# Two-layer transformer kernel: the delta rule's sums over the head dimension as two fp32r products each, and the first block's calls in a new order

## What is computed

```python
def rms_norm(x, w):
    xf = x.astype(jnp.float32)
    y = xf * lax.rsqrt(jnp.mean(xf * xf, axis=-1, keepdims=True) + EPS)
    return (y * w.astype(jnp.float32)).astype(x.dtype)

def l2_normalize(x):
    return x * lax.rsqrt(jnp.sum(x * x, axis=-1, keepdims=True) + EPS)
...
    gdn_qkv = jax.nn.silu(causal_depthwise_conv(gdn_qkv, conv_w))
    q_g, k_g, v_g = [...]                      # 4 heads of 128
    q_g = l2_normalize(q_g)
    k_g = l2_normalize(k_g)
    ...
    o_g = gated_delta_rule_chunked(q_g, k_g, v_g, g, beta)
    o_g = merge_heads(rms_norm(o_g, gdn_norm_w)).astype(x.dtype) * jax.nn.silu(gdn_gate)
```

## Time and profile before

| | |
|---|---|
| median of 3 runs | 1136.2 us (1135.94 to 1136.34) |
| the profiled execution | 1136.24 us, its span 1134.9 us |
| TensorE busy | 1110.4 us, 98% of the span |
| VectorE, ScalarE, GpSimd busy | 553.8, 566.6, 438.4 us |
| TensorE's granted clock | full speed (1.00) in the first block |

### The profile page before, as it was taken

One profiled execution on the slowest core, in us unless ns is written; L12 is line 12 of the kernel. 1 busy time (PEld: TensorE's weight loads), 2 busy tenths in 40 slices (PEclk: granted clock), 3 DMA queues, 4 the chain that ended last, 5 costly groups with the idle time before them and its releaser, 6 DMA issues.

```text
span 1134.9 us, 15124 instructions
## 1 busy us (share of the span) xinstructions
PE 1110.4 (98%) x5799; PEld 889.0 (78%) x5799; DVE 553.8 (49%) x1170; ACT 566.6 (50%) x1041; POOL 438.4 (39%) x239
## 2 busy tenths in 40 slices
PE   5999999999999999999999999999999999999997
PEld 5877877878788888788777777679888888888886
DVE  4628869779674414234255455645211114544444
ACT  5446775767777752354355555546332224333332
POOL 3133244342352444544223223325544445544441
PEclk9999999999999999999999999999999999999999
DMA  9132122121231233633222222212333333322211
GB/s 257 31 109 56 39 75 56 38 76 43 69 82 49 75 93 98 217 85 82 80 75 57 75 75 77 91 56 75 101 104 93 93 94 127 113 93 93 93 56 74
DMA packets 140379, 97.24 MB, mean 86 GB/s; under 512 B 8866, under 2 KB 124939, under 8 KB 140307
## 3 DMA queue, kind: packets, MB, share of 16 engines
q1 hardware_dynamic: 136704, 91.09, 27.5%
q10 hardware_dynamic: 3602, 5.18, 1.5%
HBM read 93.35 MB, written 2.90 MB: 85 GB/s over the span
## 4 chain that ended last, share of the span: by engine, by line
PE 93%; DVE 3%; ACT 1%; POOL 1%; issue 1%; DMA 1%; ACTq 0%; SPq 0%; DVEq 0%
PE bank L428 30%; PE bank L1154 14%; PE bank L1136 13%; PE bank L457 6%; PE bank L817 4%; PE bank L842 4%; PE bank L826 3%; PE bank L1167 2%; PE bank L926 1%; PE bank L973 1%; PE bank L957 1%; PE bank L464 1%; PE bank L640 1%; PE bank L658 1%; PE bank L583 1%; PE bank L964 1%
## 5 line engine op out<-in xcount | busy, mean ns | idle before, releaser
L2419 POOL TENSOR_TENSOR ring<-raw_ring,ring 128x1024 fp32r<-128x1024 f32 x159 | 390.0, 2457 | 597.8 <-ACT ring L1180 597.8
L428 PE MATMUL bank<-hT,ring 128*128 128x512 f32 x1536 | 402.6, 405 | 1.3 <-POOL ring L2419 1.3
L428 PEld LDWEIGHTS bank<-hT,ring 128*128 128x128 f32 x1536 | 277.8, 188 | 68.8 <-issue 15.6
L1180 ACT CAST ring<-raw_ring 128x1024 fp32r<-128x1024 f32 x160 | 167.1, 1047 | 114.3 <-PE bank L1154 90.3
L1154 PE MATMUL bank<-ring,ring_u 128*128 128x512 f32 x672 | 154.0, 391 | 0.0
L1136 PE MATMUL bank<-hT,ring 128*128 128x512 f32 x672 | 152.5, 389 | 0.0
L1154 PEld LDWEIGHTS bank<-ring,ring_u 128*128 128x128 f32 x672 | 126.2, 188 | 27.6
L1136 PEld LDWEIGHTS bank<-hT,ring 128*128 128x128 f32 x672 | 126.1, 188 | 26.1
L2393 DVE TENSOR_TENSOR ring_u<-u,ring_u 128x1024 fp32r<-128x1024 f32 x32 | 81.0, 2540 | 75.0 <-ACT ring_u L1747 75.0
L2398 DVE TENSOR_TENSOR u<-u 128x512 f32<-128x512 f32 x32 | 22.9, 715 | 139.2 <-ACT u L1754 139.2
L1754 ACT ACTIVATE u<-bank 128x512 f32<-128x512 f32 x32 | 19.1, 598 | 115.4 <-PE bank L1136 108.4
(11 more groups left out here) (290 smaller groups left out, 1511.8 us busy)
## 6 DMA issues: line engine op xcount, KB each, us to landing
raw_ring<-in_w_in SPq DMA_DIRECT2D x144, 256.0 KB, 3.3
raw_ring<-in_w_up SPq DMA_DIRECT2D x64, 256.0 KB, 3.3
raw_ring<-in_w_down SPq DMA_DIRECT2D x64, 256.0 KB, 2.7
raw_ring<-in_w_out SPq DMA_DIRECT2D x32, 256.0 KB, 2.8
x<-in_x SPq DMA_DIRECT2D x4, 512.0 KB, 5.7
raw_ring<-in_w_branch_sb SPq DMA_DIRECT2D x8, 256.0 KB, 2.9
raw_ring<-in_w_branch_gdn SPq DMA_DIRECT2D x8, 256.0 KB, 3.2
x<-in_x ACTq DMA_DIRECT2D x4, 512.0 KB, 6.3
```

The costliest lines, as they stand in the source:

```text
L428: p = pe.matmul(bank, m.slab_k8(n % 4)[:, a, k, :], m.hT[:, b, k, :], start=term == 0, stop=term == 23)
L1180: act.copy(m.ring[:, q, 0, :], m.raw_ring[:, q, :]).then_inc(s.slab_hi[q], 1)
L2419: pool.tensor_tensor(m.ring[:, q, 1, :], m.raw_ring[:, q, :], m.ring[:, q, 0, :].bitcast(F32), ALU.subtract).then_inc(s.slab_lo[q], 1)
```

## The change

Each sum becomes two fp32r products that add up in the same PSUM bank: ones x the high part of the squares, and ones x their low part. ScalarE squares straight into a tile of type fp32r: for q and o that is the place of the head's result `ogd[:, 0, i]`, for k `osb[:, 0, i]`, both free until the results are written. GpSimd squares again in float32 into a new tile `sq` and subtracts the high part into `ogd[:, 1, i]` or `osb[:, 1, i]`. TensorE waits for the new semaphore `sq_low` between the two products. Room for `sq` and the fp32r ones comes from a smaller area of small constants. And the calls of the first block stand in new places on all engines.

```diff
+        self.sq = take("sq", [P, T])
+        self.ones_r = take("ones_r", [P, P], F32R)
...
     def delta_q_sum(i):
...
-        pe.matmul(banks[6], mat["ones"], MT if i else tmp, start=True, stop=True).then_inc(s.delta_ps, 1)
+        pe.wait_ge(s.memsets, 5)
+        pe.matmul(banks[6], ones_r, m.ogd[:, 0, i, :], start=True, stop=False)
+        pe.wait_ge(s.sq_low, 6 * i + 2)
+        pe.matmul(banks[6], ones_r, m.ogd[:, 1, i, :], start=False, stop=True).then_inc(s.delta_ps, 1)
```

```diff
+        tiles.to(139)
+        delta_solve(i)
+        tiles.to(143)
+        stick_weights_T(i, 0, 3)
         tiles.to(144)
-        delta_solve(i)
-        tiles.to(147)
+        delta_chunk(i, 0)
+        tiles.to(149)
+        delta_from_state(i, 1)
+        tiles.to(150)
+        delta_chunk(i, 1)
         stick_weights_T(i, 1, 3)
-        delta_chunk(i, 0)
-        tiles.to(152)
-        stick_weights_T(i, 0, 3)
-        tiles.to(153)
-        delta_from_state(i, 1)
-        tiles.to(155)
-        delta_chunk(i, 1)
-        tiles.to(158)
+        tiles.to(151)
         delta_from_state(i, 2)
-        tiles.to(160)
         delta_chunk(i, 2)
         stick_av(i, 3)
         delta_from_state(i, 3)
-        tiles.to(162)
+        tiles.to(152)
         delta_chunk(i, 3)
-        tiles.to(169)
+        tiles.to(166)
         delta_o_sum(i)
         tiles.rest()
```

In stage 3 (merge) q sum goes from 10 to 1, decay from 22 to 12, k sum from 27 to 14, gram from 42 to 55, the levels by -10 to +0, solve from 177 to 175, chunk 3 from 219 to 217, the o sum from 224 to 229. The head's TensorE calls stay. GpSimd:

```diff
+    def low_of_squares(before, dst, x, x_ready, x_value, high_ready, high_value):
+        pool.wait_ge(x_ready, x_value)
+        if before:
+            pool.wait_ge(s.sq_low, before)
+        pool.tensor_tensor(m.sq, x, x, ALU.mult).then_inc(s.sq_low, 1)
+        pool.wait_ge(high_ready, high_value)
+        pool.wait_ge(s.sq_low, before + 1)
+        pool.tensor_tensor(dst[:, 1], m.sq, dst[:, 0].bitcast(F32), ALU.subtract).then_inc(s.sq_low, 1)
...
+    delta_q_low(0)
     delta_gates(0)
+    delta_k_low(0)
     for i in range(3):
         n = SLABS_A + 8 * (i + 1) + 2
         split(n)
         delta_masks(i)
+        delta_level(i, 4)
         split(n + 1)
-        delta_level(i, 4)
         delta_level(i, 5)
         split(n + 2)
         split(n + 3)
         delta_level(i, 6)
         split(n + 4)
         split(n + 5)
+        delta_o_low(i)
         delta_gates(i + 1)
+        delta_q_low(i + 1)
         split(n + 6)
+        delta_k_low(i + 1)
         split(n + 7)
```

`split(n + 6)` is the first slab of the next stage, `split(n + 7)` its second. In stage 3 `delta_o_low(3)` stands after the split of merge slab 10. ScalarE and VectorE:

```diff
     def delta_q_square(i):
         act.wait_ge(s.q_dve, 2 * i + 2)
-        act.activation(q_tile(i), qT, ACT.Square).then_inc(s.qk_sq, 1)
+        act.activation(m.ogd[:, 0, i, :], qT, ACT.Square).then_inc(s.qk_sq, 1)
...
     def delta_out(i):
+        act.wait_ge(s.delta_ps, 8 * i + 1)
         act.wait_ge(s.o_dve, 3 * i + 1)
-        act.activation(tmp, X, ACT.Square).then_inc(s.o_act, 1)
+        act.activation(m.ogd[:, 0, i, :], X, ACT.Square).then_inc(s.o_act, 1)
...
         tile_a(g + 5)
-        exponential(XT, s.k_dve, 2 * i + 3, s.k_sig)
-        exponential(bv, s.v_dve, 2 * i + 3, s.v_sig)
         delta_q_square(i + 1)
         stick_out(i)
         delta_out(i)
         tile_a(g + 6)
+        exponential(XT, s.k_dve, 2 * i + 3, s.k_sig)
         delta_out_high(i)
+        exponential(bv, s.v_dve, 2 * i + 3, s.v_sig)
+        tile_a(g + 7)
         delta_k_square(i + 1)
-        tile_a(g + 7)
...
+    dve.tensor_copy(m.ones_r, mat["ones"]).then_inc(s.memsets, 1)
...
         stick_soft(i, 1)
+        delta_zero(i, 4)
         delta_gram(i)
-        delta_zero(i, 4)
...
         delta_state(i, 1)
+        times(qT, qT, MT, s.q_sig, 4 * i + 8, s.q_dve)
         least(bv, PP, s.v_sig, 4 * i + 7, s.v_dve)
-        times(qT, qT, MT, s.q_sig, 4 * i + 8, s.q_dve)
         delta_state(i, 2)
         stick_out(i)
         delta_out(i)
         stick_out_low(i)
+        times(PP, PP, bv, s.v_sig, 4 * i + 8, s.v_dve)
         delta_out_low(i)
         times(kT, kT, XT, s.k_sig, 4 * i + 8, s.k_dve)
-        times(PP, PP, bv, s.v_sig, 4 * i + 8, s.v_dve)
```

More of the change, by code:

```diff
@@ L514, in tensor_program @@
     Cs, CX = (Ca, Cb), (tmp, PP)
+    ones_r = m.ones_r
     def delta_decay(i):
@@ L537, in delta_k_sum @@
             pe.wait_ge(s.small_act, 11)
-        pe.matmul(banks[5], mat["ones"], XT, start=True, stop=True).then_inc(s.delta_ps, 1)
+        pe.matmul(banks[5], ones_r, m.osb[:, 0, i, :], start=True, stop=False)
+        pe.wait_ge(s.sq_low, 6 * i + 4)
+        pe.matmul(banks[5], ones_r, m.osb[:, 1, i, :], start=False, stop=True).then_inc(s.delta_ps, 1)
     def delta_v_rows(i):
@@ L616, in delta_o_sum @@
         pe.wait_ge(s.o_act, 4 * i + 1)
-        pe.matmul(banks[5], mat["ones"], tmp, start=True, stop=True).then_inc(s.o_sum, 1)
+        pe.matmul(banks[5], ones_r, m.ogd[:, 0, i, :], start=True, stop=False)
+        pe.wait_ge(s.sq_low, 6 * i + 6)
+        pe.matmul(banks[5], ones_r, m.ogd[:, 1, i, :], start=False, stop=True).then_inc(s.o_sum, 1)
     qc, kc, vn, La, Lb, pa, pb, Csa, Csb, sgate = m.sbuf
@@ L675, in tensor_program @@
-        delta_k_sum(i)
+        tiles.to(32)
+        stick_z(i, 1)
         tiles.to(33)
-        stick_z(i, 1)
         stick_av(i, 0)
-        tiles.to(35)
+        tiles.to(34)
         delta_v_rows(i)
-        tiles.to(47)
+        tiles.to(46)
         delta_gram(i)
+        stick_weights_T(i, 0, 1)
+        tiles.to(60)
         stick_weights_T(i, 1, 1)
-        stick_weights_T(i, 0, 1)
-        tiles.to(66)
+        tiles.to(79)
+        stick_z(i, 2)
+        tiles.to(87)
         stick_av(i, 1)
-        tiles.to(75)
@@ L1405, in scalar_program @@
         g = 8 * (i + 1)
+        stick_v(i)
         delta_q_norm(i)
@@ L1471, in scalar_program @@
     merge_tile(0)
+    delta_decay(i)
     delta_k_norm(i)
-    delta_decay(i)
+    merge_tile(1)
     log_of_sigmoid(gate, m.rawg, s.g_sig, 4 * i)
-    merge_tile(1)
+    delta_mT(i)
     merge_tile(2)
-    delta_mT(i)
+    stick_v(i)
     merge_tile(3)
     stick_soft(i, 0)
-    exponential(gate, s.g_dve, 2 * i + 1, s.g_sig)
-    stick_v(i)
     stick_exp(i, 0)
@@ L1485, in scalar_program @@
     delta_level(i, 4)
+    exponential(gate, s.g_dve, 2 * i + 1, s.g_sig)
     stick_soft(i, 1)
@@ L2094, in vector_program @@
     stick_gate(i)
+    times(qg, qT, misc, s.decay_exp, 3 * i + 1, s.qg)
     delta_zero(i, 6)
@@ L2099, in vector_program @@
     delta_level(i, 6)
+    merge_least(6)
     delta_u(i)
-    times(gate, m.rawg, gate, s.g_sig, 4 * i + 4, s.g_dve)
-    times(qg, qT, misc, s.decay_exp, 3 * i + 1, s.qg)
     delta_state(i, 0)
-    merge_least(6)
     delta_state(i, 1)
@@ L2107, in vector_program @@
     merge_least(7)
+    times(gate, m.rawg, gate, s.g_sig, 4 * i + 4, s.g_dve)
     delta_state(i, 2)
@@ L2502, in gpsimd_program @@
     n = SLABS_MERGE + 2
+    split(n)
     delta_masks(i)
-    split(n)
     split(n + 1)
@@ L2508, in gpsimd_program @@
     split(n + 3)
+    split(n + 4)
     delta_level(i, 5)
-    split(n + 4)
     delta_level(i, 6)
-    for n in range(SLABS_MERGE + 7, SLABS_OUT + 8):
+    for n in range(SLABS_MERGE + 7, SLABS_MERGE + 11):
+        split(n)
+    delta_o_low(i)
+    for n in range(SLABS_MERGE + 11, SLABS_OUT + 8):
         split(n)
```

176 lines of the change are left out of this document (93 added, 83 removed).

## The result

The changed kernel takes **1138.5 us** (median of 10 runs, 1137.5 to 1140.0). The kernel before took 1135.2 beside it. The ratio is 1.0029, with a 95% interval of 1.0020 to 1.0039: 3.2 us slower, just past the 0.2% that can be told from no change. The forecast was 1134.8, 1.4 faster; the value lies inside the wide range (1131.5 to 1138.9) and outside the range of the likeliest case.

What follows compares the result with a forecast made beforehand. TensorE, busy for 98% of the span, was taken to bound the kernel. Sums saved 4.8 us, place 1 lost 1.2 and place 2 2.2: 1136.2 - 1.4 = 1134.8 us, with 8 in 10 expected within 1131.5 to 1138.9.

Steps and rivals of the forecast that it cites:

- wide range: Whole launch: the range meant to hold 8 in 10, 1131.5 to 1138.9 us.
- likeliest case: Whole launch: the forecast of 1134.8 us itself, chance 0.42, with its own range of 1134.0 to 1137.5.
- Saved: 4.8 us: First block's q, k and o sums: 12 float32 products become two fp32r each, 0.86 to 0.46 us, saving 4.8.
- Place 2: End of a stage, three times: GpSimd's new work makes the next slab's split late; net 0.75 x 3 = 2.2 us lost.
- Place 1: State chain, three stages: fewer tiles before delta_chunk, so TensorE waits for VectorE's subtraction; net 0.4 x 3 = 1.2 us lost.
- Elsewhere, -0.5 to +0.8: Stage 3 and stages outside the two places: same cover as before, within 0.5 us down and 0.8 up overall.
- The merge stage, -1.2: The merge stage (303 to 418 in the trace): expected to come down by some 1.2 us.
- VectorE starved at the stage's end: Rival, stage's end: GpSimd's operations keep VectorE out, stick_z(i, 0) comes late; 7.8 us lost, 1139.2 us, chance 0.18.
- The third rival, no single pass: The sums' products: fp32r with ones_r runs at the float32 rate, adding 12 x 0.86; 1146.5 us, chance 0.02.

Runs made afterwards that it cites:

- e1_small_area: The kernel before with only the area of small constants cut from 560 to 494 columns, no instruction changed: 1137.9 us, ratio 1.0022.
- e2_aligned: Also called the aligned kernel: the changed kernel with the area of small constants at 496 columns in place of 494: 1137.35 us, ratio 1.0015 to the kernel before.
- e6_early_cast: The aligned changed kernel with GpSimd's split of the next stage's first slab, and ScalarE's cast of that slab, moved earlier: 1135.8 us, ratio 0.9999.
- e10_level5: e9_spacing with delta_level_second(i, 5) two tiles later (113 for 111) and level 6's first half at 116 for 114: 1134.1 us, ratio 0.9983.
- e8_sums_old_place: The kernel before at 496 columns with the change's new sums and their GpSimd and ScalarE operations, every other call in its old place: 1142.6 us, ratio 1.0061.
- e9_spacing: e6_early_cast with two tiles ahead of chunks 1, 2 and 3 in stages 0 to 2, and the first stick_z at 15 for 13: 1135.1 us, ratio 0.9995.
- e12_ring_u: The kernel before with only ring_u, the stationary operand of the down projection, 32 bytes higher: 1139.3 us, ratio 1.0031.
- e5_pool_order: The aligned changed kernel with GpSimd's split of the next stage's first slab ahead of delta_gates and q's two operations: 1144.1 us, ratio 1.0077.
- e7_f32_new_place: The aligned changed kernel with the old float32 sums and without GpSimd's operations for them, calls in the new places: 1140.4 us, ratio 1.0042.

## Why the prediction was wrong

- **The layout (not in the sum).** This is the step that failed: I expected "the same cover as before" outside the two places, within 0.5 down and 0.8 up, and gave the smaller area no term, though the diff shows it. I read it as mere room. It moved the stationary operands and cost 2.5 us behind the first block (e1_small_area; 2.9 between e2_aligned and the changed kernel), gave back some 0.4 to 0.6 within it, and by itself made the launch 2.5 us longer by the medians. With it my forecast would have been 1137.3, slower than before and not faster.
- **"Saved: 4.8 us"**: held. The sums stand 0.23 apart; with `delta_decay` and `delta_k_sum` side by side they saved a restart more. In the aligned kernel the four sums with the slab cost 0.67 less a stage than before, where my terms (-1.2 and +0.75) gave 0.45.
- **Place 2, "0.75 x 3"**: right in mechanism, a little too large. In the aligned kernel waits add 0.95, 0.95 and 0.74 to the o sum with its slab (1.41, 1.41 and 1.20, less 0.46) and before they added 0.33, 0.32 and 0.29, so the net is 0.62, 0.63 and 0.45: 1.7 us in place of 2.2. e6_early_cast wins 0.76, 0.76 and 0.55 back. GpSimd's operations were 1.04 to 1.07 for x*x and 1.28 for the low part undisturbed, the two ends I had named.
- **Place 1, "0.4 x 3"**: right mechanism, wrong size: 0.76 a stage (3.18 to 3.94 in the aligned kernel), 1.1 us too little over three. I counted the waits and left out that each of them also brings a restart: the product behind a wait starts 0.21 ahead of its partner where it is 0.11 otherwise.
- **"Elsewhere, -0.5 to +0.8"**: wrong in size. I took nothing for `delta_level_second(i, 5)` and used its mechanism only for the upper end. TensorE comes two tiles sooner while ScalarE's copy keeps its distance from `delta_gram`; `stick_weights_T` in front of it grew by 0.36 a stage in the aligned kernel, and e10_level5 took 0.42 back. `stick_z` costs 0.24 a stage more and the levels' first halves 0.1; I have not tried these alone.
- **The merge stage, -1.2**: -0.8. The three sums came down by 1.3 there, but `stick_av` costs 0.38 more; that was not tried alone.
- **The rivals.** VectorE starved at the stage's end was not what made it slower: `stick_z(i, 0)` waited for nothing there. VectorE was held off, though: L2001 took 1.68 beside GpSimd's operations, against 0.69 for the same product in the earlier trace rows; L2046's 2.89 is what L2028 took before. TensorE did not come to wait for it until the stage's end ran later still (e8_sums_old_place, and a little in e9_spacing). The third rival, no single pass, did not occur; its 1146.5 also left out the 3.4 us of the two places.

The first block explains about 2.4 of the 5.2 us between the forecast and the profiled execution (1140.0), the part behind it 3.1 (2.5 to 2.9 of them the layout), less the 0.4 of the shorter head. The median of the runs is 1.6 below that execution, so by the medians the gap is 3.7.

## What to carry to other kernels

A diff that changes the size of a buffer changes the address of everything behind it: compute the addresses of TensorE's operands before and after, and put a price on the shift from a run with that edit alone. Compare the distances from start to start too, group by group, since the list of waits did not show this loss. Where TensorE is 98% busy, read every call's place as a distance in tiles to what it waits for; moving a call two tiles nearer costs the two tiles' time, and a wait costs its restart as well. When work is added to a helper engine, look at what that engine's next input waits for too: the split could only move once ScalarE's cast had.

## What the runs showed of the hardware

- A single-pass product with a 128x128 stationary operand and a 128x512 moving one takes 228.9, 231.8, 233.3, 230.0 and 232.0 ns from start to start, with the stationary operand's rows starting 0, 16, 32, 48 and 56 bytes past a multiple of 64 (moving operand at 0). The up projection, with both operands in other buffers at 0, takes 226.7, the first block's tiles, from the same two buffers, 228.9. Why, and whether the address relative to the moving operand counts, is open. The weight loads are logged at 188 ns at 0 and at 56, and at 187 in e12_ring_u.
- The pace isn't set by the address alone: products on the merged heads, at 0, stood 233.3 ns apart before a wait of TensorE and 229 behind it (before, e5_pool_order, e6_early_cast, e9_spacing, e10_level5, e12_ring_u), and 233.3 throughout where there was no wait (e2_aligned, e7_f32_new_place, e8_sums_old_place). What decides it is open.
- With the branch products, whose moving operand (osb, ogd) was the one that moved, the order is another: 233.3 ns at 0, 231.7 at 56, 231.1 at 48, 234.3 at 32 and 234.7 at 16. The better place for one product is not that for the other.
- A VectorE operation with two SBUF inputs and a GpSimd operation held each other up: VectorE's product L2001 took 1.68 us beside GpSimd's operations and 0.69 without, GpSimd's low part 1.75 in place of 1.28.
